# Input in column halves and a reordered opening; the group stage's output matmuls in two batches of four heads

## The reference, cut to what matters

```
h = rmsnorm(x, norm_mix_pre)
z, xbc, dt, q, k, v, q_idx, k_idx, w_idx, gates = split(h @ w_in)
A = ssd(z, conv(xbc), dt) @ w_ssm_out        # 64 heads in 8 groups
B = sparse_attention(q, k, v, q_idx, k_idx, w_idx) @ w_attn_out
x = x + rmsnorm((sigmoid(gA)*A + sigmoid(gB)*B) @ w_mix_out)
x = x + rmsnorm(conv_geglu(rmsnorm(x) @ w_up) @ w_down)
```

## Time and profile before

| | us |
|---|---|
| median of three runs | 1862.48 (1861.41, 1862.48, 1871.59) |
| the profiled execution, as timed | 1875.17 |
| its span in the profile | 1873.5 |
| PE busy in the span | 1826.6 (97%) |
| DVE busy | 1307.8 (70%) |
| ACT busy | 1117.3 (60%) |
| chain that ended last, share of PE | 91% |

### The profile page before, as it was taken

How to read it: one execution, slowest core, us unless ns; L and a number is a source line. 1 busy time by engine, 2 the same in 40 slices (tenths; PEclk the granted TensorE clock), 3 DMA queues, 4 the chain that set the end, 5 groups by cost and what they waited for, 6 DMA issues and landing times.

```text
span 1873.5 us, 36281 instructions
## 1 busy us (share of the span) xinstructions
PE 1826.6 (97%) x10162; PEld 1561.3 (83%) x10162; DVE 1307.8 (70%) x2520; ACT 1117.3 (60%) x2219; POOL 76.1 (4%) x137
## 2 busy tenths in 40 slices
PE   6999999999999999999999999997999999999997
PEld 5888888888888888888888888886888888887886
DVE  4766687887888788777765666655677777775554
ACT  5555566666666666677755555545666666664543
POOL 0000000110010010111100000000000000000000
PEclk9999999999999999999999999999999999999999
DMA  6656656656665665566665555665466666665664
GB/s 168 209 160 186 184 175 185 191 175 182 190 190 175 183 192 159 176 180 188 181 194 187 180 190 184 200 230 182 136 188 181 185 187 188 189 180 175 188 199 145
DMA packets 403019, 342.80 MB, mean 183 GB/s; under 512 B 28864, under 2 KB 373520, under 8 KB 402208
## 3 DMA queue, kind: packets, MB, share of 16 engines
q1 hardware_dynamic: 397792, 325.14, 58.3%
q0 software_dynamic: 4192, 16.85, 2.8%
q10 hardware_dynamic: 992, 0.30, 0.1%
HBM read 340.04 MB, written 2.16 MB: 183 GB/s over the span
## 4 chain that ended last, share of the span: by engine, by line
PE 91%; DVE 3%; ACT 3%; issue 2%; ACTq 1%; DVEq 0%
PE bank L1291 49%; PE bank L1293 24%; PE bank L1304 14%; PE bank L1309 4%; ACT w_hi L469 1%; DVE cc L956 1%; PE bank L1417 0%; DVE xc L967 0%; DVE w_lo L788 0%; ACT mix_junk L710 0%; ACT h_t L499 0%; ACTq L455 0%; DVE upad L794 0%; DVE out_t L1279 0%; ACT cc L558 0%
## 5 line engine op out<-in xcount | busy, mean ns | idle before, releaser
L788 DVE TENSOR_TENSOR w_lo<-raw,w_hi 128x512 fp32r<-128x512 f32 x1224 | 845.3, 698 | 453.3 <-ACT w_hi L469 442.9
L469 ACT ACTIVATE w_hi<-raw 128x512 fp32r<-128x512 f32 x1224 | 759.6, 629 | 448.6 <-PE bank L1293 321.9
L1291 PE MATMUL bank<-h_s,w_hi 128*128 128x512 f32 x2336 | 840.2, 403 | 1.8 <-ACT h_t L499 1.7
L1293 PE MATMUL bank<-h_s,w_lo 128*128 128x256 f32 x2336 | 654.6, 280 | 0.0
L1291 PEld LDWEIGHTS bank<-h_s,w_hi 128*128 128x128 f32 x2336 | 438.8, 188 | 113.1 <-issue 5.8
L1291 PE MATMUL bank<-o_s,w_hi 128*128 128x512 f32 x1280 | 453.5, 399 | 0.0
L1293 PEld LDWEIGHTS bank<-h_s,w_lo 128*128 128x128 f32 x2336 | 441.1, 189 | 0.6
L1293 PE MATMUL bank<-o_s,w_lo 128*128 128x256 f32 x1280 | 359.5, 281 | 0.0
L1291 PEld LDWEIGHTS bank<-o_s,w_hi 128*128 128x128 f32 x1280 | 240.6, 188 | 59.8
L1293 PEld LDWEIGHTS bank<-o_s,w_lo 128*128 128x128 f32 x1280 | 241.8, 189 | 0.0
L1291 PE MATMUL bank<-y_s,w_hi 128*128 128x512 f32 x512 | 181.2, 399 | 0.0
(11 more groups left out here) (187 smaller groups left out, 1182.3 us busy)
## 6 DMA issues: line engine op xcount, KB each, us to landing
raw<-in_w_in SPq DMA_DIRECT2D x576, 256.0 KB, 3.0
raw<-in_w_up SPq DMA_DIRECT2D x256, 256.0 KB, 3.2
raw<-in_w_ssm_out SPq DMA_DIRECT2D x128, 256.0 KB, 3.0
raw<-in_w_down SPq DMA_DIRECT2D x128, 256.0 KB, 3.3
raw<-in_w_attn_out SPq DMA_DIRECT2D x64, 256.0 KB, 2.9
raw<-in_w_mix_out SPq DMA_DIRECT2D x64, 256.0 KB, 3.5
cs_rows<-cs_dram POOLq DMA_DIRECT2D x16, 512.0 KB, 5.0
cs_rows<-cs_dram POOLq DMA_DIRECT2D x16, 256.0 KB, 6.0
```

The lines of the kernel that those rows point to most:

```text
L469: act.activation(w_hi[:, c % 4, :, :], raw[:, slot, 2 * m:2 * m + 2, :], ACT.Copy).then_inc(hi_done, 1)
L788: dve.tensor_tensor(w_lo[:, c % 4, :, :], raw[:, (c // 2) % 4, 2 * (c % 2):2 * (c % 2) + 2, :], w_hi[:, c % 4, :, :].bitcast(F32), ALU.sub ...
L1291: pe.matmul(bank[b][:], w_hi[:, w[0], w[1], w[2]], src[:, k0 + k, :], start=start and k == 0, stop=False, skip_group_check=True)
L1293: last = pe.matmul(bank[b][:, T:2 * T], w_lo[:, w[0], w[1], w[2]], src[:, k0 + k, 0:T], start=False, stop=True, skip_group_check=True)
```

## The change

The opening is built anew. `x` comes in two transfers of 1024 columns each, for all tokens, and SP issues the first weights behind it without a wait. The only parameter loaded first is the 16-row gain `mix_pre`; the other transfers move to POOL. ACT and DVE each sum the squares of 128 tokens and scale the rows of `x` by the reciprocal root in place, in four chunks of 512 columns (POOL takes the last). PE transposes the scaled rows with the identity: eight transposes ahead of half 0, and four behind each of halves 0 to 5. ACT writes the high part straight from PSUM, DVE the low part. Turn 0 now makes the first half of `v`, turn 1 the indexer's key and `dt`; the `dt` chain moves to turn 2, with its table load for Exp, and the transposes of the parameters move to turn 8. In the group stage `y_of_heads` runs as two batches, of four heads each, behind halves 29 and 37, and DVE's steps around it move.

```
+DECAYS = (20, 22, 24, 26, 28, 30, 32, 34)
+HEAD_WEIGHTS = (21, 23, 25, 27, 31, 32, 33, 35)
+Y_TILES = (30, 31, 38, 39)
+H_TURNS = [()] + [(2 * j + 4, 2 * j + 5) for j in range(1, 6)] + [(), ()]
...
-            for s in range(2):
-                sp.dma_start(x_rows[:, s, :], x_view[:, s, :]).then_inc(x_in[s], 16)
+            for n in range(2):
+                at = slice(2 * WIDE * n, 2 * WIDE * n + 2 * WIDE)
+                sp.dma_start(x_rows[:, :, at], x_view[:, :, at]).then_inc(x_in[n], 16)
...
-            for s in range(2):
-                sp.wait_ge(x_in[s], 16)
-            for n, c in enumerate((KI0, KI0, DT0, KI0 + 64)):
-                sp.dma_start(raw[:, :, :, 64 * n:64 * n + 64].rearrange("p s t c -> p (s t) c"),
-                             win[:, :, c:c + 64]).then_inc(raw_in[n], 16)
+            for m in range(4):
+                plain(win, m, V0, m, m)
+            for m in range(4):
+                slot_free(4 + m)
+                for n, c in enumerate((KI0, KI0, DT0, KI0 + 64)):
+                    sp.dma_start(raw[:, m, :, 64 * n:64 * n + 64],
+                                 win[:, 4 * m:4 * m + 4, c:c + 64]).then_inc(raw_in[m], 16)
...
+            pool.wait_ge(x_inv, 1)
+            for s in range(2):
+                pool.tensor_scalar(x_rows[:, s, 3 * X_CHUNK:D], x_rows[:, s, 3 * X_CHUNK:D], stat[:, 0, 10 + s:11 + s], None,
+                                   ALU.mult).then_inc(xn_pool, 1)
...
+            act.activation(eps[:, 2:3], eps[:, 0:1], ACT.Sqrt)
+            for n in range(2):
+                act.wait_ge(x_in[n], 16)
+                act.activation(junk[:, 0, :], x_rows[:, 0, 2 * WIDE * n:2 * WIDE * n + 2 * WIDE], ACT.Square,
+                               accum_out=stat[:, 0, 2 * n:2 * n + 1]).then_inc(x_sq, 1)
...
+            x_scaled(0)
+            split(0, 0, 0)
+            act.wait_ge(mix_out, 1)
+            for kts, q, h in (((0, 1), 1, 1), ((2, 3), 2, 2), ((4, 5), None, None)):
+                for kt in kts:
+                    h_hi_of(kt)
+                if q is not None:
+                    x_scaled(q)
+                    split(0, 0, h)
...
-                    if j == 31:
+                    if j == 34:
                         x_dt(i, 1)
-                    if 21 <= j < 37 and j % 2 == 1:
-                        weights_of_head(i, (j - 21) // 2)
-                    if j in (27, 31, 35, 39):
-                        y_tile(i, (j - 27) // 4)
+                    if j in HEAD_WEIGHTS:
+                        weights_of_head(i, HEAD_WEIGHTS.index(j))
+                    if j in Y_TILES:
+                        y_tile(i, Y_TILES.index(j))
...
+            def h_bank(kt):
+
+                if kt >= 4:
+                    pe.wait_ge(h_split, kt - 3)
+                if kt % 4 == 0:
+                    if kt < 12:
+                        pe.wait_ge(xn_act, kt // 4 + 1)
+                        pe.wait_ge(xn_dve, kt // 4 + 1)
+                    else:
+                        pe.wait_ge(xn_pool, 2)
+                for s in range(2):
+                    last = pe.transpose(bank[4 + kt % 4][:, P * s:P * s + P], x_rows[:, s, P * kt:P * kt + P], ident[:])
+                last.then_inc(h_mm, 1)
...
-                        if j in (26, 30, 34, 38):
-                            y_of_heads(i, (j - 26) // 4)
+                        if j in (29, 37):
+                            for q in range(2):
+                                y_of_heads(i, (j - 29) // 4 + q)
```

More of the change, by code:

```diff
@@ L298, in plain @@
             def plain(w, m, c, u, s):
[L300 removed]
+                if not isinstance(u, int) or u >= 4:
+                    slot_free(u)
                 for k in (1, 0):
@@ L446, in _ @@
             link, linked = links.link, links.linked
[L447 to L460, removed]
+            act.dma_start(mix_rows[:], rows_of(norm_mix_pre)).then_inc(mix_in, 16)
             def split(i, per, c):
@@ L487, in _ @@
[L487 to L504, removed]
+            def x_scaled(q):
+                at = slice(X_CHUNK * q, X_CHUNK * q + X_CHUNK)
+                act.activation(x_rows[:, 0, at], x_rows[:, 0, at], ACT.Copy,
+                               scale=stat[:, 0, 10:11]).then_inc(xn_act, 1)
@@ new lines, in _ @@
+            act.wait_ge(x_sums, 1)
+            act.activation(stat[:, 0, 8:10], stat[:, 0, 6:8], ACT.Sqrt, scale=1.0 / D, bias=eps[:, 0:1]).then_inc(x_rms, 1)
+            act.wait_ge(x_inv, 1)
+            x_scaled(0)
[7 more added lines that the diff above has]
+                    split(0, 0, h)
@@ L507, in _ @@
                     h = 8 * p + j
+                    if p == 0:
+                        for kt in H_TURNS[j]:
+                            h_hi_of(kt)
                     split(0, 0, h + LEAD)
-                    if p == 1 and j == 1:
+                    if p == 2 and j == 0:
+                        act.wait_ge(small_in, 32)
+                        act.activation(small[:, 2:3], small[:, 1:2], ACT.Exp).then_inc(dt_step, 1)
+                    if p == 2 and j == 1:
                         act.wait_ge(dt_step, 3)
@@ L522, in _ @@
                         act.activation(rel[:, c % 2, :], bank[5 + c % 2][:, 0:3 * P], ACT.Relu).then_inc(misc_read, 1)
+                    if p == 8 and j == 2:
+                        act.wait_ge(par_mm, 1)
+                        act.activation(par[:, KT:4 * P], bank[6][:, KT:4 * P], ACT.Copy)
+                        act.activation(par[:, 4 * P:PAR_ROWS], bank[7][:, 0:PAR_ROWS - 4 * P], ACT.Copy)
+                        act.activation(par[:, 5 * P:PAR_COLS], bank[7][:, P:P + 32], ACT.Copy).then_inc(par_out, 1)
                 for t in range(2):
@@ L695, in load_root @@
             def load_root():
-                act.activation(eps[:, 4:6], eps[:, 2:4], ACT.Sqrt)
+                act.activation(eps[:, 4:5], eps[:, 0:1], ACT.Sqrt)
             load_root()
@@ new lines, in _ @@
+            linked()
+            dve.wait_ge(x_sq, 2)
+            dve.tensor_tensor(stat[:, 0, 6:8], stat[:, 0, 0:2], stat[:, 0, 2:4], ALU.add).then_inc(x_sums, 1)
+            dve.wait_ge(x_rms, 1)
+            dve.reciprocal(stat[:, 0, 10:12], stat[:, 0, 8:10]).then_inc(x_inv, 1)
+            dve.wait_ge(x_inv, 1)
+            x_scaled(0)
+            dve.wait_ge(mix_out, 1)
+            for kts, q, h in (((), None, 0), ((0, 1), 1, 1), ((2, 3), 2, 2), ((4, 5), None, None)):
+                for kt in kts:
+                    h_lo_of(kt)
+                if q is not None:
+                    x_scaled(q)
+                if h is not None:
+                    lo(0, 0, h)
@@ L1346, in _ @@
                     half(0, 0, 8 * p + j, h_s, 2 * j, b, b + 1, j == 0)
+                    if p == 0 and j < 6:
+                        for kt in (2 * j + 4, 2 * j + 5):
+                            h_bank(kt)
                     if (p, j) in ((2, 2), (3, 2)):
```

158 lines of the change are left out of this document (86 added, 72 removed).

## The result

The changed kernel takes 1853.83 us, the median of 10 runs (1848.93 to 1861.99). The kernel before, run beside it, takes 1863.51 us (10 runs, 1860.36 to 1871.59). The ratio is 0.995, with a 95% interval from 0.9936 to 0.9963. The change is 9.7 us faster by the medians. The forecast was 10.9.

A forecast was written before the change was run, and what follows sets the result against it. PE, once started, hardly waits; the start's 11.0 us parameter wait and PE's work between halves bound it. Terms -10.4 + 0.2 + 0.7 - 1.4 = -10.9 us take 1862.5 to 1851.6, range 1845 to 1859.

The forecast's parts named there:

- a transfer of `x` that lands after 10: Start of the kernel: a second transfer of `x` landing after 10 us would show the forecast wrong.
- Opening: Kernel start up to half 8: half 0 starts at 13.6, half 8 at 29.6 instead of 40.04, -10.4 us.
- I keep this for the second half of columns: Opening, arrival of `x`: the second transfer, issued at 1.3, takes 7.4 us as before and lands at 8.7.
- weights or `x` late: Rival, opening: first weights take bandwidth from `x`, up to 4.5 us later; opening -7.3, time 1854.7; chance 0.14.
- The steps of 1.85: Turn 0, while `x` is transposed: one half and four transposes take 1.41 + 0.44 = 1.85 us, PE setting the pace.
- The rise of the clock: Opening: PE's clock rises 3.8 us after the first matmul, counted from 13.6, so at 17.4.
- Clock stays low in turn 0: Rival, turn 0: the clock rises only at 26; opening -6.3, time 1855.7, or 1857 without group savings; chance 0.18.
- Turn 2: The moved `dt` chain with its Exp table load, and DVE's copy of `v`: +0.2 us, between 0 and 1.5.
- Parameters: Turn 8: four full and two small transposes of the parameters between halves, +0.7 us, between 0.5 and 1.1.
- Group stage: Two batches side by side save 0.09, twice in each of eight groups: -1.4 us, between 0 and -2.9.
- Stalls in the group stage: Rival: DVE falls past its lead, PE waits in every group; 1873.8 us, chance 0.04; milder, 1857.8, 0.06.
- I know of no part of the change that scales with that excess: Sum: the profiled execution's 12.7 us above the median was left out, and -10.9 us applied to the median.

The follow-up runs named there:

- experiment 4: Changed kernel with `x` in two transfers of 128 tokens each (8 KB pieces), ACT summing the first, DVE the second: 1851.93 us.
- experiment 3: Changed kernel, but SP waits for both transfers of `x` before it issues the first weights, as before: 1853.67 us.
- experiment 8: Kernel of experiment 7 plus 24 float32 matmuls of constants on PE while it waits for `x`: 1849.27 us.
- experiment 7: Kernel of experiment 4, with ACT also summing half of the columns of the second 128 tokens: 1847.8 us.
- experiments 1 and 6: Changed kernel with the group stage of before, 1864.98 us; changed kernel with one half between the two batches of each pair, 1860.64 us.

## Why the prediction was right, and where it was not

The sign, the range and the median hold: 1853.83 against 1851.6, within 1845 to 1859. That the sum came within 2.2 us of the median is in part luck: it was 3.4 us short of what the traces show of the change, and something that it did not know made up for it. Two of its terms were off in opposite directions, and one of its own signs of being wrong came true, a transfer of `x` that lands after 10.

- **Opening, -10.4 forecast, -9.2 traced** at half 8 (40.04 to 30.84). The mechanism is right; the term was mis-sized at its first bullet, "I keep this for the second half of columns". `x` is complete at 10.6 and not at 8.7, because column halves move at 218 GB/s where token halves move at 352 (experiment 4). That is 1.9 late, and half 0 is 2.1 late (15.66 against 13.6). The rival "weights or `x` late" named the right symptom and the wrong cause: experiment 3 takes the weights away, and `x` stays late.
- Of the 2.1, 0.9 came back in turn 0: half 2 stands at 20.42, 1.2 behind the forecast's 19.2, and half 8 at 30.84, 1.2 behind its 29.6. The forecast let the clock rise at 17.4, and PE's records are short from 17.75, so a later half 0 spends less of its time at the low clock: from half 0 to half 8 the change takes 15.18 us, 0.70 more than experiment 8 with the clock up. The price of the low clock was put at 1.7 us for a half 0 at 13.6; experiment 7, with half 0 at 13.29, pays 1.57. The steps of 1.85 are exact. The 29.6 itself lies 0.2 above the forecast's own steps, which end at 29.4; halves 6 and 7 took 1.50 and 1.51 instead of 1.41, which hid that.
- **The rise of the clock, 17.4 forecast, 18.0 traced,** is a hit by luck. The forecast took 3.8 us from PE's first matmul, and then counted from half 0 (13.6) and not from its own first transpose (11.3), which would have given 15.1. And the 3.8 was misread: "the next 48 take 6.33, 0.13 each" is a mean over both levels. In the kernel before, PE's busy time and records with `x` are, up to 20.52, up to 22.02, and behind it:

```profile
16.57:20.52 3.95, 3.78 (x16) 1.00 0.94 153
20.52:22.02 1.50, 1.50 (x7) 1.00 0.00 0
22.02:26.85 4.83, 4.83 (x43) 1.00 0.36 109
```

The seven behind 20.52 still take 0.21 each, those behind 22.02 0.11, and the trace's first entry of the clock starts at 22.02. That is 5.45 us behind the first matmul with `x`; in the second profile of the same kernel the entry starts at 19.94, and in the change at 18.00, 4.6 us behind the first transpose.
- **Clock stays low in turn 0** did not happen: the records were short from 17.75, within half 0 (in experiment 7 from 17.5, within half 1), and the steps with transposes behind half 2 took 1.84 to 1.86 in all of them.
- **Turn 2, +0.2 forecast, about +0.1 traced.** One gap of 0.20 where 0.11 is usual, right behind DVE's chain. The table load costs no drain: Exp starts 1.29 us after the load's start in turn 2 as well (43.55 to 44.84). The Trainium skill, "ScalarE: Activation LUTs", section "What ACT_TABLE_LOAD costs", has 1.38 of drain beside the load; the trace doesn't agree in either kernel.
- **Parameters, +0.7 forecast, +0.79 and 0.09 behind it traced**, within its bounds. From half 8 to the last `q_t` 1.0 us of the opening's 9.2 are given back, which is these and turn 2. Opening, turn 2 and parameters: -9.5 forecast, -8.2 traced.
- **Group stage, -1.4 forecast, -6.1 traced.** This is the step that failed: "Bounds: 0.98 for the second batch if nothing is saved, 0.80 if both changes are." The lower bound was no bound. It counted the time from a batch's first record to the next half (470.31 to 471.11), and that holds the batch's return to the halves, which a second batch behind it pays instead. Nor is the batch's first matmul as long behind another batch. The second batch costs 0.66, so a pair saves 0.32 and not 0.09, and a group's period falls from 65.5 to 64.8, by 0.7 and not 0.2. Two pairs in eight groups make 5.1 of the 6.1. The last 1.0, 0.1 a group, isn't settled: S takes 530.0 to 530.5 in the six profiles with this group stage, and 535.5 to 536.2 in the four without its pairs, so part of it is how much S differs between executions. Of the other batches, `x_tok` alone costs 0.36 + 0.08, as forecast.
- **Stalls in the group stage** did not come. PE waited for `w_lo` 0.2 us in all.

The change's own part is thus -14.3 us in the traces, where the sum had -10.9. The median fell by 9.7, and its interval, 6.9 to 11.9, doesn't hold 14.3. What fits the difference is PE's two paces: O and M take about 389 or 394 us and U 344.0 or 350.6, by the execution, for every kernel here. The profiled execution of the change, 1854.61, had the slow pace in O and M alone, and eight of its ten runs lie at 1852.77 to 1855.17. The second profile of before, 1862.95, had neither, and the lower five of before's ten runs lie at 1860.36 to 1862.61. Two such executions differ by 14.3 - 5.1 = 9.2. That is an estimate: the pace of a run that was not profiled is not on record. Single runs do fall into groups; experiment 4's, in order of size, are 1848.34, 1848.37, 1848.76 and then 1855.09, 1855.25, 1857.08. A median of ten such runs can stand a step of 5 to 7 us off.

The forecast's own sentence on this, "I know of no part of the change that scales with that excess", was right, and the excess of 12.7 us of the profiled execution was for the most part both slow paces (5.1 + 6.6 = 11.7, and the second profile of the same kernel is 12.2 shorter). Not settled is in what share of the runs each pace comes, and whether the code has a hand in that share: with the new opening O and M were slow in two profiles of seven, with the old one in one of three, which tells nothing.

## What to carry to other kernels

Where batches of the same kind of matmul stand between streams, put them side by side: what a batch costs alone holds a lead-in and a return, and only one of each is paid for a pair. Don't count on it for batches of different kinds; transposes beside a batch saved nothing here. When a large transfer is cut to have its first part sooner, cut it so that each partition's piece stays whole. Then look at the last landing: here what was left to do behind it set the start, and not what was left behind the first. Before a difference of some us is put down to an edit, compare marks at the ends of stages that the edit did not touch: here they moved by 6.6 us without it.

## What the runs showed of the hardware

- TensorE has two steady paces at a full granted clock and with no wait: a pair of a 512-wide and a 256-wide matmul takes 0.3467 or 0.3533 us (279.41 us for 806 pairs after, 279.84 for 792 before, between 1360 and 1640 us). It keeps one for a whole stage of 200 us or more, and takes either in different executions of one kernel. O and U can differ within an execution. What decides it stays open; it was not tried.
- Transfers of 1 MB whose pieces are 4 KB for each partition moved 218 GB/s from 2 to 6 us, with the DMA engines 0.93 busy, and those of 8 KB pieces 352 at 0.91 (experiment 4).
- A batch of four float32 matmuls (eight records) between two streams of halves costs PE 0.98 us, and 0.66 directly behind another such batch. Directly behind four transposes it still costs 0.98 to 0.99.
- The moment at which PE's records grow short is not fixed for one code: with half 0 at 15.66, 15.56 and 15.50 (after, experiments 1 and 6, the same opening), half 1 came 2.91, 3.44 and 3.43 us later. The traces' first entries of the granted clock start at 18.00, 19.14 and 18.94.
- Up to its first entry a trace says nothing of the granted clock, and the windows show 1.00 there: in the change's first 18 us they read 1.00 beside 512-wide records of 0.63 to 0.80 us, which take 0.40 later.
